# Reordered first loads, roundings and parameter steps, and the RG-LRU gate chain split in two, in a one-core decoder kernel

## What is computed

```python
u = rmsnorm(x, ln_mix) @ w_in             # xa, ga, qb, fb, ib, gb
xc = conv_b + sum(xpad[:, j:j + T] * conv_w[j] for j in range(4))
r, ig = sigmoid(xh @ w_ra + b_ra), sigmoid(xh @ w_rx + b_rx)
log_a = -8 * r * softplus(-lam);  a = exp(log_a)
bt = sqrt(-expm1(2 * log_a)) * ig * xc    # (a first-token term for h0)
hs = scan(h = a * h + bt);  y_a = hs * gelu(ga)
o = hgrn2(silu(qb) * 128**-0.5, k, v, log f);  y_b = rms(o) * gn * silu(gb)
x = x + concat(y_a, y_b) @ w_out
x = x + square(relu(rmsnorm(x, ln_mlp) @ w_up)) @ w_down
y = rmsnorm(x, ln_final)
```

## Time and profile before

| | |
|---|---|
| median of 3 runs | 2497.25 us |
| the profiled execution, its own time | 2496.15 us |
| its span | 2494.5 us |
| TensorE busy / weight loads busy | 2396.7 us / 2147.5 us |
| VectorE / ScalarE / GpSimd busy | 940.7 / 632.5 / 284.3 us |
| mean granted TensorE clock | 0.986 |
| DMA queue of ScalarE / SyncE / GpSimd | 31.03 / 151.01 and 100.68 MB in all, packets in q10, q1, q0 |

### The profile page before, as it was taken

How to read it: one execution, slowest core, us unless ns; L and a number is a source line. 1 busy time by engine, 2 the same in 40 slices (tenths; PEclk the granted TensorE clock), 3 DMA queues, 4 the chain that set the end, 5 groups by cost and what they waited for, 6 DMA issues and landing times.

```text
span 2494.5 us, 38619 instructions
## 1 busy us (share of the span) xinstructions
PE 2396.7 (96%) x15842; PEld 2147.5 (86%) x15842; DVE 940.7 (38%) x1593; ACT 632.5 (25%) x1189; POOL 284.3 (11%) x276
## 2 busy tenths in 40 slices
PE   5999999999999999999899999999999999999995
PEld 4777777788888888888798899899999999999995
DVE  6665664421121121223765666534211211211224
ACT  4344344321131120222334234422201201201210
POOL 0000001212212212222000000000100000010010
PEclk9999999999999999999999999999999999999998
DMA  5323234344444444454432222232232222222223
GB/s 178 120 99 105 102 103 169 128 150 150 128 151 151 127 151 151 129 203 151 121 101 76 69 69 86 81 136 85 86 100 84 84 98 87 84 90 95 84 84 109
DMA packets 88145, 284.10 MB, mean 114 GB/s; under 512 B 15856, under 2 KB 19056, under 8 KB 88048
## 3 DMA queue, kind: packets, MB, share of 16 engines
q1 hardware_dynamic: 41472, 151.01, 18.6%
q0 software_dynamic: 27648, 100.68, 12.5%
q10 hardware_dynamic: 18928, 31.03, 3.5%
HBM read 171.07 MB, written 111.62 MB: 113 GB/s over the span
## 4 chain that ended last, share of the span: by engine, by line
PE 91%; DVE 5%; ACT 2%; ACTq 1%; issue 1%; DVEq 0%
PE bank L438 29%; PE bank L440 28%; PE bank L439 28%; PE aux L572 1%; PE aux L500 1%; DVE a_lo L1272 1%; ACT s_in L637 1%; PE aux L528 1%; PE aux L551 1%; PE aux L550 1%; DVE xc L1230 1%; PE aux L505 1%; DVE xy L1005 0%; DVE xy L1159 0%; PE aux L451 0%
## 5 line engine op out<-in xcount | busy, mean ns | idle before, releaser
L438 PE MATMUL bank<-a_hi,w_hi 128*128 128x358 f32 (+3 forms) x2560 | 923.3, 361 | 38.3 <-DVE a_lo L1272 20.4
L439 PE MATMUL bank<-a_lo,w_hi 128*128 128x358 f32 (+3 forms) x2560 | 906.4, 354 | 0.0
L440 PE MATMUL bank<-a_hi,w_lo 128*128 128x358 f32 (+3 forms) x2560 | 906.2, 354 | 0.0
L438 PEld LDWEIGHTS bank<-a_hi,w_hi 128*128 128x128 f32 x2560 | 485.6, 190 | 88.8 <-POOL w_lo L393 22.5
L440 PEld LDWEIGHTS bank<-a_hi,w_lo 128*128 128x128 f32 x2560 | 486.3, 190 | 43.6
L439 PEld LDWEIGHTS bank<-a_lo,w_hi 128*128 128x128 f32 x2560 | 486.2, 190 | 43.4 <-issue 2.2
L438 PE MATMUL bank<-b_hi,w_hi 128*128 128x358 f32 (+3 forms) x1280 | 452.1, 353 | 0.0
L439 PE MATMUL bank<-b_lo,w_hi 128*128 128x358 f32 (+3 forms) x1280 | 450.6, 352 | 0.0
L440 PE MATMUL bank<-b_hi,w_lo 128*128 128x358 f32 (+3 forms) x1280 | 450.4, 352 | 0.0
L1360 DVE TENSOR_TENSOR xy<-xy,bank 128x356 f32 (+5 forms) x160 | 94.1, 588 | 559.3 <-PE bank L440 559.3
L637 ACT ACTIVATE a_hi<-tmp 128x356 f32 (+5 forms) x160 | 88.3, 552 | 830.5 <-DVE tmp L1349 830.5
(11 more groups left out here) (159 smaller groups left out, 1414.0 us busy)
## 6 DMA issues: line engine op xcount, KB each, us to landing
w_st<-in_wall SPq DMA_DIRECT2D x96, 512.0 KB, 4.3
kept_hi<-w_hi SPq DMA_DIRECT2D x96, 512.0 KB, 5.1
kept_lo<-w_lo SPq DMA_DIRECT2D x96, 512.0 KB, 5.9
w_hi<-kept_hi POOLq DMA_DIRECT2D x96, 512.0 KB, 3.9
w_lo<-kept_lo POOLq DMA_DIRECT2D x96, 512.0 KB, 4.6
xs<-in_xT ACTq DMA_DIRECT2D x8, 536.0 KB, 6.7
xy<-in_xT ACTq DMA_DIRECT2D x8, 536.0 KB, 7.9
xs<-in_xT ACTq DMA_DIRECT2D x16, 256.0 KB, 6.6
```

The costliest lines, as they stand in the source:

```text
L438: pe.matmul(ps, wh, xh, start=(j == 0), stop=False)
L439: pe.matmul(ps, wh, xl, start=False, stop=False)
L440: mm = pe.matmul(ps, wl, xh, start=False, stop=(j == 7))
```

## The change

1. First loads: SyncE now issues weight block 0, x blocks 1, 3, 5, 7 of tile 0, weight block 1, the same x blocks of tile 1, and the three constants; ScalarE issues only the parameters and the even x blocks. TensorE's wait for the constants goes from RS to the first GATE and the first VT.
2. Roundings: ScalarE rounds weight block 1 after the eight `a_hi` of tile 0, not before. It takes a root of one column (`sink`) ahead of the squares.
3. Parameter steps: the two small exponentials come after RS on ScalarE. On VectorE `rest_of_prep` and, in pass 0, the two memsets come after the convolution of head 0. The wait for the mask DMAs (`smp_in`) comes after RS.
4. Gate chain: VectorE's GATE becomes GA (u, a, v, igx) and GB (bt to the end), at slots 18 and 0 of the next iteration in pass 0, at 27 and 1 in pass 1. ScalarE's square root goes to GA's slot.

The diff, cut:

```diff
+GATE_A_SLOT, GATE_B_SLOT = [18, 27], [0, 1]
...
+                    if i < HEADS and s == GATE_A_SLOT[p]:
+                        pieces.append(("GA", i))
+                    if i >= 1 and s == GATE_B_SLOT[p]:
+                        pieces.append(("GB", i - 1))
...
-            for j in range(2):
-                load(j, j)
+            load(0, 0)
+            for b in range(1, KB, 2):
+                load_x0(0, b)
+            load(1, 1)
+            for b in range(1, KB, 2):
+                load_x0(1, b)
+            sync.dma_start(ident[:, :], ident_d).then_inc(const_in, 16)
+            sync.dma_start(w_ra[:, :, :], wra_d).then_inc(const_in, 16)
+            sync.dma_start(w_rx[:, :, :], wrx_d).then_inc(const_in, 16)
...
             for t, (c0, w) in enumerate(TILES[0]):
-                for b in range(KB):
+                for b in range(0, KB, 2):
                     act.dma_start(xs[:, b, c0:c0 + w], xT[b, :, c0:c0 + w]).then_inc((x_in2 if t else x_in)[b], 16)
-            act.dma_start(ident[:, :], ident_d).then_inc(const_in, 16)
-            act.dma_start(w_ra[:, :, :], wra_d).then_inc(const_in, 16)
-            act.dma_start(w_rx[:, :, :], wrx_d).then_inc(const_in, 16)
...
+                elif name == "GA":
                     act.wait_ge(rg_step, rg_at(p, i, "v"))
                     fn(ea[:, 0:TH[p]], ea[:, 0:TH[p]], ACT.Sqrt, scale=-1.0).then_inc(rg_act, 1)
...
-            for n in range(2):
-                round_weights(n)
+            round_weights(0)
             act.wait_ge(par_in, 16)
-            act.wait_ge(prep, 3)
-            fn(sp[:, 0, :], sp[:, 0, :], ACT.Exp, scale=-1.0).then_inc(prep_act, 1)
-            fn(lbv[:, 0, :], lbv[:, 0, :], ACT.Exp).then_inc(prep_act, 1)
...
+                    if p == 0 and t == 0:
+                        round_weights(1)
                 if p == 0:
+                    act.wait_ge(consts, 5)
+                    fn(sink[:, :], eps[:, :], ACT.Sqrt)
                     input_squares(0)
...
-                elif name == "GATE":
+                elif name == "GA":
+                    a = AUX[(p, "GATE", i)]
                     dve.wait_ge(rg_act, 2 * n + 1)
...
+                elif name == "GB":
                     dve.wait_ge(rg_act, 2 * n + 2)
+                    T, E, I = ta[:, 0:th], ea[:, 0:th], ig[:, 0:th]
                     rg(p, i, "bt", tt(I, I, E, ALU.mult))
...
                         add_input_square(0, b)
-                    rest_of_prep()
...
+                        if un == (0, XA, nt - 1) and p == 0:
+                            rest_of_prep()
+                            dve.memset(near[:, :, :], 0.0)
+                            dve.memset(attn[:, :], 0.0).then_inc(zeroed, 1)
+                            dve.wait_ge(zeroed, 1)
```

More of the change, by code:

```diff
@@ L157, in aux_uses @@
 def aux_uses(p, name):
-    if name in ("FN", "FY", "R", "N", "Y"):
+    if name in ("FN", "FY", "R", "N", "Y", "GA", "GB"):
         return 0
@@ L217, in build @@
         eps = sb("eps", [P, 1])
+        sink = sb("sink", [P, 1])
         sp = sb("sp", [P, 4, 4])
@@ L369, in keep, with load_x0 @@
                 sync.dma_start(kept_lo[m], w_lo[:, slot, :].bitcast(F32)).then_inc(w_kept[slot], 16)
-            for j in range(2):
-                load(j, j)
+            def load_x0(t, b):
+                c0, w = TILES[0][t]
+                sync.dma_start(xs[:, b, c0:c0 + w], xT[b, :, c0:c0 + w]).then_inc((x_in2 if t else x_in)[b], 16)
+            load(0, 0)
[7 more added lines that the diff above has]
+            sync.dma_start(w_rx[:, :, :], wrx_d).then_inc(const_in, 16)
             with sync.Fori(0, BLOCKS // 2 - 1) as i:
@@ L463, in piece @@
                     pe.wait_ge(consts, 5)
-                    pe.wait_ge(const_in, 16 * 3)
                     pe.wait_ge(x_acc, KB * (p + 1))
@@ L470, in piece @@
                 elif name == "VT":
+                    if n == 0:
+                        pe.wait_ge(const_in, 16 * 3)
                     for t in range(NT[p]):
@@ L592, in _ @@
                     for name, i in pieces:
-                        if name not in ("FN", "FY", "R", "N", "Y"):
+                        if name not in ("FN", "FY", "R", "N", "Y", "GA", "GB"):
                             piece(p, name, i)
@@ L871, in _ @@
                         started = True
+                        if p == 0:
+                            act.wait_ge(prep, 3)
+                            fn(sp[:, 0, :], sp[:, 0, :], ACT.Exp, scale=-1.0).then_inc(prep_act, 1)
+                            fn(lbv[:, 0, :], lbv[:, 0, :], ACT.Exp).then_inc(prep_act, 1)
                     if half:
@@ L876, in _ @@
                     for name, i in pieces:
-                        if name not in ("RS", "FN", "R", "OT", "Y"):
+                        if name not in ("RS", "FN", "R", "OT", "Y", "GB"):
                             piece(p, name, i)
@@ L1276, in _ @@
                         add_input_square(0, b)
-                    rest_of_prep()
                 dve.wait_ge(x_ready, tile_no(p, NT[p] - 1, KB - 1))
[L1279 to L1282, removed]
+                if p:
+                    dve.memset(near[:, :, :], 0.0)
+                    dve.memset(attn[:, :], 0.0).then_inc(zeroed, 1)
+                    dve.wait_ge(zeroed, p + 1)
                 dve.wait_ge(consts, 5)
@@ L1297, in _ @@
                         started = True
+                        dve.wait_ge(smp_in, 16 * (8 + 11 * p))
                     if half:
@@ L1312, in _ @@
                     for name, i in pieces:
-                        if name not in ("RS", "NF"):
+                        if name not in ("RS", "NF", "GATE"):
                             piece(p, name, i)
```

## The result

The changed kernel takes 2478.84 us in the median of 4 runs (2478.54 to 2482.93), the kernel before, beside it, 2497.19 us (4 runs): ratio 0.9931, 95% interval 0.9919 to 0.9943. That is 18.35 us or 0.73% faster. The prediction said 2486.9 us, 10.3 us faster, with a range from 2483.5 to 2492.5. The direction was right; the gain was 8 us larger than forecast and lies outside the range. The profiled execution of the changed kernel took 2482.93 us, span 2481.3 us, 4.1 us more than the other three; that difference is in pass 1 and is taken up at the end of the experiments.

A forecast was written before the change was run, and what follows sets the result against it. TensorE, busy 2396.7 of 2494.5 us, bounds the kernel, so only its waits can be won. RS -6.9, parameter steps +2.1 and pass 0's heads -5.6 give -10.4 us: 2486.9 us in the median, range 2483.5 to 2492.5.

The forecast's parts named there:

- The start: First loads and roundings: with fewer loads issued by ScalarE, the last `a_lo` ends 5.5 us earlier, at 22.95 us.
- (a): Rival at the start: x data lands late and paces TensorE; gain there shrinks to about 3 us, 2491; chance 0.15.
- (e): Rival at the start: a stop in the first unit keeps TensorE at the lower clock; 2500.5 us; chance 0.02.
- RS: TensorE resumes after RS at 47.3 us instead of 54.19, 6.9 us earlier, 5.5 of it from the start.
- Parameter steps: Moved ahead of block 4's split on VectorE, 6.0 us of work with 3.9 us of cover: 2.1 us later, once.
- The head's end, pass 0: D's 2.03 us wait goes, L1 waits 0.6 us: net 1.4 us a head, 5.6 us for four.
- Pass 1: Head ends of pass 1, where D does not wait: zero gain, between -0.5 and +1 us a head.
- the sum: Whole kernel: RS -6.9, parameter steps +2.1, pass 0's head ends -5.6, together -10.4 us.
- (b): Rival at pass 0's head ends: the wait moves whole from D to L1, heads give 0; 2492.5 us; chance 0.1.
- (c): Rival on ScalarE, between q's two sigmoids in pass 0: costlier table switches make it slower, 2501 us; chance 0.04.
- (d): Rival at block 4 or L1: parameter steps cost nothing or L1 never waits; -12.5 to -13, 2484 us; chance 0.14.

The follow-up runs named there:

- e8: The changed kernel with the parameter steps and memsets behind block 4's split on VectorE; 2476.81 us, 2.2 us below the changed kernel beside it.
- e7: The changed kernel with the gate chain in one piece at its old slot and without the tile `sink`; 2492.42 us against 2497.69 for the kernel before.
- e13: The kernel before with the gate chain split in pass 0 alone; 2487.61 us, -9.4 us, ratio 0.9962.
- e1: The kernel before with one unused 4-byte tile behind `eps`, no instruction changed; 2493.04 us against 2496.52, ratio 0.9986.
- e14: The kernel before with the gate chain split in pass 1 alone; 2496.38 us, -0.6 us, ratio 0.9999.
- e15: The kernel before with the gate chain split in both passes, run again beside the two halves; 2486.09 us, -10.9 us, ratio 0.9962.
- e6: The kernel before with the gate chain split in both passes and nothing else, first run; 2485.45 us, -12.2 us, ratio 0.9950.
- e4: The kernel before with an unused tile of 20 bytes, no instruction changed; 2492.71 us, -3.8 us, ratio 0.9985.

## Why the prediction was wrong

- **The start: right.** Predicted: table load after 5.4 us, `w_hi` 0 at 6.7, last `a_lo` at 22.95. Measured: 5.70, 6.99 and 23.18; the first matmul came at 11.25 and not at 10.8. VectorE's two stops for GpSimd's splits stayed (the first `a_lo` took 2.33 us and the seventh 2.88, the others 0.74), data kept up, and rivals (a) and (e) fell.
- **RS: right, a little small.** "6.9 us earlier": it was 7.5, TensorE at 46.71. The stretch at the lower level after it, which "I leave as long as it was", ended at 50.6 instead of 59.4 us, 3.9 us long and not 5.2; that gave another 0.6.
- **Parameter steps: right.** "2.1 us later, once": a wait of 2.0 us on `w_lo` at block 4. e8 got it back. With RS the forecast had -4.8 us, the run alone (e7) measured -5.3.
- **The head's end, pass 0: the wait right, its price too low; the first step that failed.** "Net 1.4 us a head, 5.6 us for four": by the waits, 8.1 - 2.8 = 5.3. But the split of pass 0 alone measured -9.4. "The wait of 2.03 us goes" priced the wait and not the stretch at 1.2 GHz that followed it in half of the cases. The profile before had one of the four, at head 3, and I did not look: 336.92 and 338.20 have matmuls of 0.63 us there. e13's interval, -6 to -13 us, is too wide to show the 3.2 us by itself; they rest on the counts of the profiles and on the 8.8 us between the traces.
- **Pass 1: right.** Zero forecast, -0.6 us (interval of both signs) measured.
- **The second step that failed is a term missing in the sum, "-10.4 us".** It had a term for what each moved instruction does and none for what a new tile does. `sink` was taken for free; it moved `b_hi` and `b_lo` onto a multiple of 16 bytes, -3.5 us (e1). With -5.3 (e7), -9.4 (e13), -0.6 (e14) and -3.5 (e1) the parts add up to -18.8 us against -18.35, -18.7 and -17.7 measured. Each of them has an error of 2 us or more, so this agreement is partly luck: with the split of both passes (e15 -10.9, e6 -12.2) in place of e13 and e14 the sum is -19.7 or -21.0. Of the 8 us by which the forecast was short, 3.8 are at the heads (9.4 for 5.6), 3.5 the tile and 0.5 the start.
- **The rivals.** (b) fell: L1 waits 0.6 to 1.0 us, not 2. (c) fell: ScalarE has 57 table loads for 48, 1283 ns each, and in 37 of the 57 cases the next activation starts 0.01 us after it (the others start 0.4 us or more after it, for data). (d) fell at block 4 and at L1. The range was made of these alone, so nothing in it could reach 2479; neither of the two terms that were missing is a wait.

## What to carry to other kernels

A declaration is an edit, too: add up the bytes ahead of each large operand of TensorE before and after, and keep its start on a multiple of 16; here that is worth 3.5 us for no instruction at all. A wait of TensorE of about 2 us can cost more than its length (here 1.6 us more after half of them): look at the durations of the matmuls right behind it in several executions, and put the mean of that into the price of removing such waits. And where the medians of two versions differ by less than the step between two clock patterns (4 us here), compare the traces stretch by stretch, since the medians may only say which pattern was met more often.

## What the runs showed of the hardware

- Matmuls of 512 and 496 columns (pass 0's MLP) whose `b_hi` or `b_lo` starts 12 bytes past a multiple of 16 follow one another every 0.2296 us (mean of the distances between starts over pass 0's 1536 in the kernel before), at a multiple of 16 every 0.2273 us (e1, e4): 1%. The Trainium skill, SBUF — State Buffer, "Specifications (TRN2)", gives SBUF lines of 16 bytes, with a penalty for each step to a new one. The runs agree with that, but only starts 0 and 12 bytes past a multiple of 16 were tried, so a unit of 8 bytes would fit them as well, and the mechanism was not tested. In pass 1's MLP, tiles of 358 columns, the spacing is 0.164 us at either place.
- The granted clock fell for 3.4 us after 12 of 24 waits of 2.0 us, and after none of those of 1.3 us or less at pass 0's head ends; the wait of 2.0 us at block 4 was followed by such a stretch in four of the seven profiles that have it.
